# A hybrid GLA and convolution block: the mixer's schedule rewritten, conv tiles in two pairs, taps placed between VectorE's other steps

## The reference

```python
xn = rmsnorm(h, norm1_g);  proj = xn @ w_in            # q, k, v, g, z, c_in, c_gate
log_a = log_sigmoid(z @ w_gate_up + b_gate) / 16
o_gla = rmsnorm(gla_chunked(q, k, v, log_a), gla_norm_g) * silu(g)   # 4 heads, causal, with decay
u = causal_depthwise_conv(c_in * sigmoid(c_gate), conv_w, conv_b)    # width 31, 512 channels
o_conv = silu(channel_group_norm(u, conv_norm_g, conv_norm_b))       # 8 groups
h = h + concat(o_gla, o_conv) @ w_out
h = h + relu(rmsnorm(h, norm2_g) @ w_mlp_in) ** 2 @ w_mlp_out
out = rmsnorm(h, final_norm_g)
```

## Time and profile before

| | us |
|---|---|
| median of 3 runs | 2461.77 |
| lowest, highest | 2454.72, 2462.40 |
| the profiled execution's own time | 2464.16 |
| its span, first to last instruction | 2462.4 |
| TensorE busy in the span | 2265.6 |
| VectorE, GpSimd, ScalarE busy | 1277.9, 815.1, 697.3 |
| mixer, MLP (by the first MLP load) | 998, 1464 |

### The profile page before, as it was taken

How to read it: one execution, slowest core, us unless ns; L and a number is a source line. 1 busy time by engine, 2 the same in 40 slices (tenths; PEclk the granted TensorE clock), 3 DMA queues, 4 the chain that set the end, 5 groups by cost and what they waited for, 6 DMA issues and landing times.

```text
span 2462.4 us, 27807 instructions
## 1 busy us (share of the span) xinstructions
PE 2265.6 (92%) x10192; PEld 1847.5 (75%) x10192; DVE 1277.9 (52%) x2117; ACT 697.3 (28%) x997; POOL 815.1 (33%) x710
## 2 busy tenths in 40 slices
PE   7758988997899798699999999999899999999998
PEld 6546766776777676488888888888688888888887
DVE  4956588757857783434343333434633433334335
ACT  3334424253234224321212212123422122121222
POOL 6473466436423631212222221223322222212222
PEclk9878988998999899799999999999999999999999
DMA  7532345543454354711111111121331111111111
GB/s 256 183 128 103 121 140 175 206 154 129 145 182 160 112 163 170 272 36 52 51 51 51 36 49 51 51 84 49 132 112 51 51 51 42 44 50 51 51 34 69
DMA packets 148519, 252.25 MB, mean 102 GB/s; under 512 B 9792, under 2 KB 91744, under 8 KB 148448
## 3 DMA queue, kind: packets, MB, share of 16 engines
q1 hardware_dynamic: 148448, 251.34, 30.7%
HBM read 205.17 MB, written 46.14 MB: 102 GB/s over the span
## 4 chain that ended last, share of the span: by engine, by line
PE 55%; DVE 2%; DMA 1%; ACT 1%; POOL 1%; issue 0%; POOLq 0%; SPq 0%; ACTq 0%; DVEq 0%
PE ps L68 9%; PE ps L69 9%; PE ps L70 9%; PE ps L1692 9%; PE ps L1693 9%; PE ps L1694 9%; DVE hn L1592 1%; DMA hn<-h_dram 1%; DVE h_sb L1629 0%; DVE hT_lo L1601 0%; POOL m_rstd L1485 0%; ACT m_junk L1536 0%; PE ps L1665 0%; DVE h_sb L1607 0%; DMA h_sb<-h_dram 0%
## 5 line engine op out<-in xcount | busy, mean ns | idle before, releaser
L1489 POOL TENSOR_TENSOR m_lo<-raw,m_hi 128x1024 fp32r<-128x1024 f32 x128 | 305.9, 2412 | 1029.5 <-ACT m_hi L1545 1029.5
L1629 DVE TENSOR_TENSOR h_sb<-ps,h_sb 128x512 f32<-128x512 f32 x512 | 349.8, 690 | 273.6 <-PE ps L1694 270.2
L68 PE MATMUL ps<-hT_hi,m_hi 128*128 128x512 f32 x1024 | 400.0, 391 | 7.3 <-POOL m_lo L1489 4.1
L1692 PE MATMUL ps<-m_hi,ff_hi 128*128 128x512 f32 x1024 | 400.4, 391 | 6.0 <-DVE h_sb L1629 5.3
L69 PE MATMUL ps<-hT_lo,m_hi 128*128 128x512 f32 x1024 | 399.8, 390 | 0.0
L70 PE MATMUL ps<-hT_hi,m_lo 128*128 128x512 f32 x1024 | 399.5, 390 | 0.0
L1694 PE MATMUL ps<-m_hi,ff_lo 128*128 128x512 f32 x1024 | 399.4, 390 | 0.0
L1693 PE MATMUL ps<-m_lo,ff_hi 128*128 128x512 f32 x1024 | 399.4, 390 | 0.0
L920 DVE SCALAR_TENSOR_TENSOR y_sb<-u_sb,cw_col,y_sb 128x512 f32<-128x512 f32 x480 | 369.6, 837 | 0.2
L1616 DVE TENSOR_TENSOR relu<-relu 128x512 f32<-128x512 f32 x128 | 88.5, 692 | 484.9 <-ACT relu L1552 484.9
L1545 ACT ACTIVATE m_hi<-raw 128x1024 fp32r<-128x1024 f32 x128 | 128.2, 1049 | 540.4 <-PE ps L1694 524.8
(11 more groups left out here) (165 smaller groups left out, 2887.3 us busy)
## 6 DMA issues: line engine op xcount, KB each, us to landing
wt<-w_kept SPq DMA_DIRECT2D x168, 512.0 KB, 3.3
...
```

The costliest lines, as they stand in the source:

```text
L68: nc.tensor.matmul(out, w_hi, x_hi, start=first, stop=False)
L1489: nc.gpsimd.tensor_tensor(m_lo[:, i, :], raw[:, i, :], m_hi[:, i, :].bitcast(F32), ALU.subtract).then_inc(m_lo_ok, 1)
L1629: nc.vector.tensor_tensor(h_sb[:, t, c], ps[:, 4 + n % 4, :], h_sb[:, t, c], ALU.add).then_inc(add_ok, 1)
L1692: nc.tensor.matmul(o, ff_hi[:, i, r], m_hi[:, FT + i, c], start=(i == 0), stop=False)
```

## The change

One list of steps for the whole mixer (`mixer_steps`) takes the place of the lists for each kind of block. What it does:

- The conv branch is worked off in two pairs of channel tiles, 0 and 1, then 2 and 3. The norm of pair 0 starts in the middle of its block (`CN0`), that of pair 1 in the last conv tiles (`CN1`), and its products (`cn_rstd`, `cn_sig`, `cn_mixed` of pair 1) stand in the q and k steps of the next block.
- The first tap of each tile (`first_tap`) and the affine (`cn_sig`) move from VectorE to ScalarE. VectorE keeps 480 taps.
- `TAP_PLAN` gives the number of taps in front of each of VectorE's steps. In blocks 2 and 3: 15 in front of gate 0, 9 in front of gate 1, 14 in front of `decay`; in front of the second chunk's `gla_expo`, in the v steps, 26 in blocks 1 and 3, and 3 and 19 in block 2. Block 0 has none in the first conv phase, then 13, 11 and 15, and in the v steps 14 and 18.
- A selection takes all four heads: four levels, then three levels and the diagonal, so eight `copy_predicated` a chunk. TensorE's score matmuls are ordered to match.
- The copy of `qe_head` is a step of its own (`gla_heads`), one g tile after v, and the first `gla_scores` of a block follows that tile. The last `gla_scores` and `gla_out` of block 0 stand in block 1's q and k steps; those of block 3 after its last output unit. The x rows of block 1 are all loaded and scaled during block 0's v and g steps.
- g tiles and x rows swap banks; `v` writes banks 4 and 5 first and waits for the last k tile only at its third bank.
- Three raw weight stages in place of four; a bfloat16 scratch of its own for the squares.

```diff
-STAGES = 4
+STAGES = 3
...
+TAP_STEPS = TAPS - 1
+ALL_TAPS = TAP_STEPS * CT
+PAIR_TAPS = 2 * TAP_STEPS
+DVE_STEPS = ("make_wz", "conv_in", "gate", "decay", "gla_expo", "gla_select", "gla_out", "x_norm", "x_tr", "g", "out_done",
+             "cn_mean", "gn_rstd", "cn_rstd", "cn_sig", "cn_mixed")
+GLA_AT = {0: (16.3, 7.2), NB - 1: (16.5, 6.6)}
...
+def gla_events(b):
+    events = [(8, ("gla_expo", 0)), (9.5, ("gla_factors", 0))] + [(10 + 1.3 * i, ("gla_decayed", 0, i)) for i in range(3)]
+    start, period = GLA_AT.get(b, (16.5, 7.8))
+    for c in range(TT):
+        o = start + period * c
+        if c + 1 < TT:
+            events += [(o + 0.1, ("gla_expo", c + 1))]
+        events += [(max(o - 1, 16), ("gla_heads", c))]
+        events += [(o + 0.8, ("gla_scores", c, 0)), (o + 0.8, ("gla_select", c, 0))]
+        if c + 1 < TT:
+            events += [(o + 1.8, ("gla_factors", c + 1))]
+        events += [(o + 3.0, ("gla_scores", c, 1)), (o + 3.0, ("gla_select", c, 1))]
+        if c + 1 < TT:
+            events += [(o + 3 + 1.4 * i, ("gla_decayed", c + 1, i)) for i in range(3)]
+        events += [(o + 4.4, ("gla_out", c))]
+    o = events[-1][0]
+    events += [(o + 1, ("gn_square",)), (o + 2.8, ("gn_sum",)), (o + 4, ("gn_rstd",))]
+    return [(u, e, b) for u, e in events]
...
+    head = [("z",), take("qk", 0, 2), ("gate", 0), take("qk", 1, 2), ("gate", 1), take("qk", 2, 2),
+            ("decay",), take("qk", 3, 2)]
+    fill = head + [take("v", k, 1) for k in range(KT)]
+    fill += [("v_done", 2 * 4 + KT - 1)]
+    fill += [take("g", h, 2) for h in range(HEADS)]
...
+    ev = over + gla_events(b)
+    if mix:
+        ev += [(0.8, ("cn_rstd", 1), b - 1), (1.6, ("cn_sig", 1), b - 1), (3.0, ("cn_mixed", 1), b - 1)]
+        ev += [((13.2 + 1.2 * h if b == 1 else 4 + 1.4 * h), ("gn_mixed", h), b - 1) for h in range(HEADS)]
+    if nxt:
+        ev += [(8 + i, ("x_sq", i), b) for i in range(2)] + [(12 + i, ("x_norm", i), b) for i in range(2)]
+        late, scale = (26.6, 29) if mix else (12, 16)
+        ev += [(late + i, ("x_sq", 2 + i), b) for i in range(2)] + [(scale + i, ("x_norm", 2 + i), b) for i in range(2)]
+    ev += [((20 if b == 1 else CN0[kind]) + u, (n, 0), b) for u, n in zip((0, 1.8, 3.3), ("cn_mean", "cn_var", "cn_rstd"))]
+    ev += [(CN0[kind] + 8, ("cn_sig", 0), b), (CN0_MIX[kind], ("cn_mixed", 0), b)]
+    if nxt:
+        ev += [(CN1[kind] + u, (n, 1), b) for u, n in zip((0, 1.8), ("cn_mean", "cn_var"))]
+    ev.sort(key=lambda e: e[0])
...
+CN0 = {"start": 28.5, "body": 17.5, "end": 17.5}
+CN0_MIX = {"start": 38, "body": 40.2, "end": 40.2}
+CN1 = {"start": 36.5, "body": 52.5}
...
+def add_taps(steps):
+    out = []
+    ready, mixed = set(), {(-1, 0), (-1, 1)}
+    todo = [(m, p, i) for m in range(NB) for p in range(2) for i in range(PAIR_TAPS)]
+    plan = list(TAP_PLAN)
+    def emit(n):
+        while n > 0:
+            m, p, i = todo[0]
+            k = min(n, PAIR_TAPS - i)
+            out.append((("taps", p, i, k), m))
+            del todo[:k]
+            n -= k
+    for step, b in steps:
+        name = step[0]
+        if on_dve(step, b):
+            emit(plan.pop(0) if plan else 0)
+        if name == "conv_in" and b >= 0:
+            emit(sum(1 for m, p, i in todo if m < b or m == b and p <= step[1] // 2))
+        if name == "cn_mean":
+            emit(sum(1 for m, p, i in todo if m < b or m == b and p <= step[1]))
+        out.append((step, b))
+        if name == "cn_mixed":
+            mixed.add((b, step[1]))
+        if name == "conv_in" and step[1] % 2 == 1:
+            ready.add((b + 1, step[1] // 2))
+        for m, p in sorted(ready):
+            if (m - 1, p) in mixed:
+                out.append((("first_tap", p), m))
+                ready.discard((m, p))
+    assert not todo and not ready
+    return out
...
+TAP_PLAN = [
+    0, 0, 0, 0, 0, 13, 11, 15, 0, 0, 0, 14, 18, 0, 0, 0, 0, 4, 5, 1, 6, 0, 0, 0, 0, 0, 6, 0, 1, 4,
+    6, 0, 0, 0, 5, 11, 0, 0, 0, 0, 6, 0, 6, 1, 14, 2, 0, 0, 0, 26, 0, 0, 0, 2, 6, 10, 0, 9, 0, 0,
+    0, 3, 6, 4, 0, 3, 0, 2, 0, 2, 0, 10, 4, 4, 0, 0, 0, 0, 0, 1, 0, 6, 0, 15, 9, 14, 0, 0, 3, 19,
+    0, 0, 0, 2, 2, 5, 1, 6, 0, 0, 0, 3, 6, 4, 0, 0, 3, 0, 0, 0, 0, 9, 4, 6, 2, 0, 0, 0, 0, 1,
+    0, 6, 0, 15, 9, 14, 0, 26, 0, 0, 0, 2, 2, 5, 1, 6, 2, 2, 10, 4, 4, 1, 0, 4, 6, 0, 0, 0, 0, 0,
+    0, 0, 0, 0, 0, 0,
+]
...
+                elif name == "first_tap":
+                    if first(b):
+                        act.wait_ge(consts_ld, CONSTS)
+                    for j in pair(step):
+                        act.wait_ge(u_ok, b * 2 * CT + 2 * j + 2)
+                        if not first(b):
+                            act.wait_ge(cn_lo, b * CT - CT + j + 1)
+                        nc.scalar.activation(y_sb[:, j, :], u_sb[:, j, 0:BLK], ACT.Identity, bias=cb_col[:, j:j + 1],
+                                             scale=cw_col[:, j, 0:1]).then_inc(tap0_ok, 1)
...
+                elif name == "cn_sig":
+                    if b > 0 and step[1] == 0:
+                        act.wait_ge(silu_ok, (b + 1) * HEADS)
+                    for j in pair(step):
+                        act.wait_ge(cn_n, b * CT + j + 1)
+                        nc.scalar.activation(cn_gate(b, j), y_sb[:, j, :], ACT.Sigmoid, bias=cnb_col[:, j:j + 1],
+                                             scale=cg_col[:, j:j + 1]).then_inc(cn_sig, 1)
+                    for j in pair(step):
+                        act.wait_ge(cn_sig, b * CT + j + 1)
+                        nc.scalar.activation(y_sb[:, j, :], y_sb[:, j, :], ACT.Identity, bias=cnb_col[:, j:j + 1],
+                                             scale=cg_col[:, j:j + 1]).then_inc(cn_aff, 1)
...
+            def tap(m, p, i):
+                k, j = 1 + i // 2, 2 * p + i % 2
+                if i < 2:
+                    dve.wait_ge(tap0_ok, m * CT + j + 1)
                 else:
-                    dve.wait_ge(tap_ok, m * ALL_TAPS + i - 1)
-                    nc.vector.scalar_tensor_tensor(out=y_sb[:, j, :], in0=u_sb[:, j, k:k + BLK],
-                                                   scalar=cw_col[:, j, k:k + 1], in1=y_sb[:, j, :],
-                                                   op0=ALU.mult, op1=ALU.add).then_inc(tap_ok, 1)
...
+                    done = (b * TT + c) * (NL + 1) + part * HALF_LEVELS
+                    for i, lv in enumerate(SCORE_LEVELS[part]):
+                        s = LEVELS[lv]
                         n = P // (2 * s)
-                        dve.wait_ge(probs_ok, n0 + lv + 1)
-                        dst = probs[:, hh, :].rearrange("p a (n h s) -> p a n h s", h=2, s=s)[:, :, :, 1, :]
-                        src = acc[:, 2 + lv // 4, lv % 4 * P:lv % 4 * P + P].rearrange("p (a n s) -> p a n s", a=2, s=s)
+                        if i > 0:
+                            dve.wait_ge(probs_ok, done + i)
+                        dst = probs[:, :, :].rearrange("p a (n h s) -> p a n h s", h=2, s=s)[:, :, :, 1, :]
+                        src = acc[:, 2 + i // 2, i % 2 * KEY:i % 2 * KEY + KEY].rearrange("p (a n s) -> p a n s", a=HEADS, s=s)
                         msk = lvl_mask[:, lv, :].bitcast(I32).rearrange("p (n s) -> p n s", s=s)
-                        nc.vector.copy_predicated(dst, msk.unsqueeze(1).broadcast_to([P, 2, n, s]),
+                        nc.vector.copy_predicated(dst, msk.unsqueeze(1).broadcast_to([P, HEADS, n, s]),
                                                   src).then_inc(probs_ok, 1)
+                    if part == 1:
+                        dve.wait_ge(probs_ok, done + len(SCORE_LEVELS[1]))
+                        diag = acc[:, 3, DIAG:DIAG + HEADS].unsqueeze(2).broadcast_to([P, HEADS, P])
+                        nc.vector.copy_predicated(probs[:, :, :],
+                                                  ident[:, :].bitcast(I32).unsqueeze(1).broadcast_to([P, HEADS, P]),
+                                                  diag).then_inc(probs_ok, 1)
...
-G_BANK = [1, 0, 1, 0]
-X_BANKS = [(4, 5), (0, 1), (0, 1), (4, 5)]
-OUT_BANK = [(4, 5, 0, 1), (0, 1, 4, 5)]
+G_BANK = [4, 5, 4, 5]
+X_BANKS = [(0, 1), (4, 5), (0, 1), (4, 5)]
+OUT_BANK = [(0, 1, 4, 5), (0, 1, 4, 5)]
+CONV_BANK = [(0, 1)] * CT
 LAST_OUT_BANK = [(0, 1, 2, 3), (6, 7, 4, 5)]
-V_BANK = [1, 0, 4, 5]
+V_BANK = [4, 5, 1, 0]
 GN_BANK = [2, 3, 6, 7]
-DIAG = (NL - 4) * P
-CN_BANK = [4, 5, 4, 5]
+DIAG = KEY
+PARTS = 2
+SCORE_LEVELS = [(0, 1, 2, 3), (4, 5, 6)]
+HALF_LEVELS = len(SCORE_LEVELS[0])
```

430 lines of the change are left out of this document (175 added, 255 removed).

## The result

The changed kernel takes 2441.26 us (median of 6 runs, 2436.3 to 2446.68) against 2461.81 us for the kernel before, measured beside it: ratio 0.9922 with a 95% interval of 0.9902 to 0.9942, so 20.5 us. The forecast was 58 us (2404). The direction was right and the range (2335 to 2466) holds the time; the size was wrong by almost two thirds.

What follows compares the result with a forecast made beforehand. TensorE, busy 92% of the span, was taken to lose time to mixer waits and the low clock after them. From 2464.2 us, -40 - 12 - 8 - 6 + 8 = -58 gave 2406, less 2.4 for the median: 2404; range 2335 to 2466.

Steps and rivals of the forecast that it cites:

- the wait for qe_head in blocks 2 and 3: TensorE's wait at the first scores: 15 to 20 us if taps hold k_end, 5 if not; 9 to 10 taken.
- Block 0: First mixer block: 40 us less (20 to 60), from 22 up to the second score group and 18 after.
- the rest of the block: Block 0's smaller waits and low clock, about 28 us, of which 18 were to be saved.
- That is 13 us with one answer: Block 0, before conv_in: without 48 early taps the 10.17 us wait and about 3 us of low clock go.
- Block 1: Second mixer block: 12 us less, with smaller waits for qe_head and silu_g, after 5 us for ScalarE's queue.
- Rival 2: VectorE bounds g to the last output unit; three blocks lose 10 us each: 2434 us; 0.12 including no effect.
- The selection: VectorE's score selection: 1.7 to 2.1 us less per chunk, 16 times, about 30 us, credited only for work order.
- ScalarE's new queue: Block heads: pair 1's conv norm waits for GpSimd ahead of the q copy; 5 us a block, bounds 0 and 15.
- rival 3: ScalarE waits behind GpSimd behind taps, delaying q and k copies: 30 us in each of three blocks, 2494 us; chance 0.13.
- Rival 1: GpSimd gets past VectorE's taps promptly: 20 us more saved in block 0, 8 per later block; 2360 us, chance 0.30.
- The tail: After block 3's last output unit: last gla_out and norm chain uncovered, about 20 us; 8 us slower (0 to 15).
- Three stages for four: Raw weight stages: load and split fit within three units, so 0 us, up to 5 if GpSimd falls behind.

Runs made afterwards that it cites:

- The memsets: Changed kernel with a one-column VectorE memset behind every third tap of all tap runs in all blocks: 2423.0 us, measured twice.
- the kernel with two-head copies: Changed kernel with each four-head masked copy of the score selection split into two copies of two heads: 2443.5 us.
- memsets in these runs: Changed kernel with a one-column memset behind every third tap, only in the runs that hold k_end in blocks 2 and 3: 2428.1 us.

## Why the prediction was wrong

By the medians 37 us of the forecast are missing. The memsets, which take away the hold and move nothing, give 18 of them back, so the largest failed step is the wait for qe_head in blocks 2 and 3, taken at 9 to 10 us where the hold made it 15.5 and 15.9. The second is block 1, whose new deadlines for VectorE had no price; its cause is shown in part only.

Against the profiled executions the forecast was -58 and came out at -27.9, 30 us short: 7 in block 0, 11 in block 1, 4 in block 2, 7 in block 3 with the tail, 1 in the MLP.

**Block 0** (forecast -40, measured -32.5). The chain up to the first g tile was followed rightly: the run of 14 taps was to hold k_end for 9.3 us and leave a wait of 17 us for the weights, and it is 9.83 and 14.35; the first g tile was to end near 149, and the first scores, which stand right behind it, start at 146.65. TensorE gets through the same 18 weight units in 79.1 us from z in place of 102.5: 23.4 gained, 22 forecast. What failed is the rest of the block: 18 forecast, 32.5 - 23.4 = 9 measured. Right behind the second g tile stands a wait of 8.15 us for probs, where the kernel before has none over 2.9, and the working has no term for it; with memsets in all runs it is still 8.5, so it isn't the hold's. The split of the 40 into causes failed too. "That is 13 us with one answer" had no such answer: taken by itself, removing the early taps gives nothing. The wait of 10.17 us was TensorE waiting early for VectorE's work instead of late; the same taps then delay the factors. What pays 17 to 21 us is the other end: 33 taps stand in late steps and not in front of the factors and the selections.

**Block 1** (forecast -12, measured -1). This is the term that was most mis-sized. I took the waits of before (qe_head, silu_g) down one by one. I did not place the two new deadlines in VectorE's queue: the mean of pair 0 at unit 20 in place of after the last output unit, and block 0's gn_mixed among the v steps. v_sb (8.1), y_sb (5.6) and probs (5.4) took what qe_head (11.4) and silu_g (9.2, still 4.5) gave. That the mean is such a deadline shows where 8 of its taps were put behind the first selection: y_sb went from 5.6 to 11.7. Why the taps come too late for it, beside GpSimd's chain or by their number, stays open: 20 taps fewer gave 6 of the 11 us. Rival 2 had the form of it, in the wrong place: VectorE binds ahead of the mean; its load from g to the last output unit was not tested, since the kernel with two-head copies added 5 us and not 20.

**Blocks 2 and 3, qe_head** (forecast a wait of 9 to 10). k_end was held 15.1 and 15.4 us, within the 17 I gave as a bound; the wait was 15.5 and 15.9, the bad end of my range, with 7.9 more at chunk 1 of block 3, which the memsets leave as it is. The failed step is "I take 9 to 10, between them": the run's length decided, and a mean of two cases is neither. With memsets in these runs, nothing else changed, the wait is 8.9 and 8.5, block 2 gains 10.6 over before (forecast 8) and block 3 with the tail loses 2.2 (forecast 2). So in these two blocks the hold is more than the whole error of 11 us: it cost 6.6 and 6.8.

**The selection** (about 30 us of VectorE by my sum): it was 90.5 us and is 70.7, 20 less. A four-head copy takes 525 ns where I took 444. I had credited nothing for it by itself, so the sum does not change.

**ScalarE's new queue** (5 us a block). The waits for q_sb are 1.8 us in each of blocks 2 and 3; the term was too big, and rival 3's mechanism is real: it appeared at 6.6 us as soon as a run of taps met the hand-over.

**Rival 1** (the port passes promptly, 2360) held in one block of four. GpSimd arrived 0.1 (blocks 0 and 1), 1.3 and 2.5 us into a run. It was held in block 0 and let in in block 1, so early arrival does not decide. The rule of the Trainium skill (SBUF — State Buffer, Who interferes with whom) that the exclusion lasts one instruction fits the 0.91 us products of block 1 and disagrees with 9.8, 15.1 and 15.4 us. And getting in is not free: both engines then take longer (0.91 us for 0.45, 0.89 for 0.67), and even the kernel with k_end free everywhere is at 2423, not 2360.

**The tail** (+8): 22.8 us uncovered for the 18 forecast, with the mechanism as described. **Three stages for four** (0 us) was not tried alone, so its price stays open.
